# A hybrid decoder trunk in split fp32: weight tiles moved 64 bytes up, and 104 instead of 128 weight columns for the gate unit

## The reference, cut to what matters

```python
def hybrid_layer(x, p_i, ...):
    h = rmsnorm(x, norm_mix)
    z = h @ w_in                     # 1024 x (4*384 + 256 + 4*384 + 2*4)
    (rq, rk, rv, rg, pu, mq, mk, mv, mo, mi, mf) = jnp.split(z, offs, axis=-1)
    y_ret, y_pool, y_ml = retention(...), pool_mix(...), mlstm(..., mi, mf, ...)
    x = x + jnp.concatenate([y_ret, y_pool, y_ml], axis=-1) @ w_out
    h = rmsnorm(x, norm_ffn)
    gu = h @ w_gate_up               # 1024 x 5632
    x = x + (jax.nn.silu(gu[..., :D_FF]) * gu[..., D_FF:]) @ w_down
    hp = rmsnorm(x, norm_ple)
    return x + jax.nn.sigmoid(hp @ w_ple_gate) * (p_i @ w_ple_proj)
```

## Time and profile before

| What | Value |
|---|---|
| Median of 3 runs | 2496.22 us |
| Span of the profiled execution | 2494.5 us |
| What lies around the span, against the median | 1.7 us |
| TensorE matmul busy | 2467.6 us (99%), 11768 records |
| TensorE weight loads busy | 2037.2 us (82%) |
| VectorE, ScalarE, GpSimd busy | 1270.7, 898.2, 992.5 us (51%, 36%, 40%) |
| TensorE in the chain that ended last | 97% |
| Mean granted TensorE clock | 0.998 of full |

### The profile page before, as it was taken

One profiled execution on the slowest core, in us unless ns is written; L12 is line 12 of the kernel. 1 busy time (PEld: TensorE's weight loads), 2 busy tenths in 40 slices (PEclk: granted clock), 3 DMA queues, 4 the chain that ended last, 5 costly groups with the idle time before them and its releaser, 6 DMA issues.

```text
span 2494.5 us, 29698 instructions
## 1 busy us (share of the span) xinstructions
PE 2467.6 (99%) x11768; PEld 2037.2 (82%) x11768; DVE 1270.7 (51%) x1760; ACT 898.2 (36%) x1298; POOL 992.5 (40%) x596
## 2 busy tenths in 40 slices
PE   7999999999999999999999999999999999999998
PEld 6888888888888888888878887888888888888886
DVE  7967845543343352333596777545433433423335
ACT  4333334433333341125333252344433333322253
POOL 3211112278877832321221121223788877222120
PEclk9999999999999999999999999999999999999999
DMA  4342222123223252211143322311232223422111
GB/s 164 105 98 65 71 85 85 45 84 92 76 77 91 87 195 107 78 50 44 38 154 98 78 56 67 102 59 60 80 93 81 76 85 110 150 110 70 51 49 70
DMA packets 89370, 214.43 MB, mean 86 GB/s; under 512 B 34568, under 2 KB 43016, under 8 KB 84880
## 3 DMA queue, kind: packets, MB, share of 16 engines
q1 hardware_dynamic: 61456, 126.90, 16.9%
q10 hardware_dynamic: 27776, 85.63, 10.0%
HBM read 163.70 MB, written 35.68 MB: 80 GB/s over the span
## 4 chain that ended last, share of the span: by engine, by line
PE 97%; DVE 1%; ACT 1%; issue 0%; DMA 0%; POOL 0%; ACTq 0%; DVEq 0%; POOLq 0%
PE proj L1986 20%; PE proj L1987 20%; PE proj L1988 20%; PE proj L2090 5%; PE aux L2090 5%; PE aux L2089 5%; PE proj L2089 5%; PE aux L2088 5%; PE proj L2088 5%; PE aux L2205 1%; PE aux L2224 1%; PE aux L2215 1%; PE aux L2310 0%; PE aux L2315 0%; PE aux L2281 0%; PE aux L2268 0%
## 5 line engine op out<-in xcount | busy, mean ns | idle before, releaser
L1937 POOL TENSOR_TENSOR w_lo<-w_raw,w_hi 128x1024 fp32r<-128x1024 f32 (+1 forms) x144 | 367.2, 2551 | 1256.5 <-ACT w_hi L1468 1256.4
L1986 PE MATMUL proj<-h_hi,w_hi 128*128 128x512 f32 x1760 | 694.8, 395 | 0.9 <-POOL w_lo L1937 0.9
L1988 PE MATMUL proj<-h_lo,w_hi 128*128 128x512 f32 x1760 | 685.5, 389 | 0.0
L1987 PE MATMUL proj<-h_hi,w_lo 128*128 128x512 f32 x1760 | 685.1, 389 | 0.0
L1986 PEld LDWEIGHTS proj<-h_hi,w_hi 128*128 128x128 f32 x1760 | 330.4, 188 | 72.4 <-issue 3.1
L1988 PEld LDWEIGHTS proj<-h_lo,w_hi 128*128 128x128 f32 x1760 | 330.3, 188 | 69.2
L1987 PEld LDWEIGHTS proj<-h_hi,w_lo 128*128 128x128 f32 x1760 | 330.5, 188 | 68.8 <-issue 2.4
L1468 ACT ACTIVATE w_hi<-w_raw 128x1024 fp32r<-128x1024 f32 (+1 forms) x143 | 146.5, 1026 | 440.5 <-PE proj L1988 295.9
L1025 DVE TENSOR_TENSOR x<-x,proj 128x512 f32<-128x512 f32 x128 | 87.7, 687 | 405.6 <-PE proj L1988 405.3
L1944 POOL TENSOR_TENSOR w_lo<-w_raw,w_hi 128x512 fp32r<-128x512 f32 x120 | 183.5, 1531 | 88.5 <-ACT w_hi L1450 88.5
L1944 POOL TENSOR_TENSOR w_lo<-turns,w_hi 128x512 fp32r<-128x512 f32 x120 | 180.4, 1504 | 62.9 <-ACT w_hi L1450 62.9
(11 more groups left out here) (290 smaller groups left out, 4161.3 us busy)
## 6 DMA issues: line engine op xcount, KB each, us to landing
w_raw<-weights SPq DMA_DIRECT2D x168, 512.0 KB, 3.7
act_spill<-act ACTq DMA_DIRECT2D x44, 512.0 KB, 5.5
turns<-weights SPq DMA_DIRECT2D x40, 512.0 KB, 4.4
h_whole<-act_spill ACTq DMA_DIRECT2D x12, 1024.0 KB, 8.1
ffn_b_whole<-act_spill ACTq DMA_DIRECT2D x8, 1024.0 KB, 5.5
w_raw<-weights SPq DMA_DIRECT2D x16, 384.0 KB, 3.1
ml_d<-rows_spill ACTq DMA_DIRECT2D x64, 64.0 KB, 3.4
rows<-ret_qkv ACTq DMA_DIRECT2D x32, 128.0 KB, 2.3
```

The source lines that it names most:

```text
L1937: g.tensor_tensor(wlo[:, slot, 0:n], w, whi[:, slot, 0:n].bitcast(F32), ALU.subtract).then_inc(weights_ready.sem, 1)
L1986: pe.matmul(out, wh, rhi, start=first, stop=False)
L1987: pe.matmul(out, wl, rhi, start=False, stop=False)
L1988: return pe.matmul(out, wh, rlo, start=False, stop=final)
```

## The change

Two edits. A tile of 16 columns (64 bytes) is allocated between `w_raw` and `w_hi`, so `w_hi`, `w_lo` and all that is allocated behind them (`const`, `par`, `early`, `rstd`, `turns`, `rows`, `small` and the rest) begin 64 bytes further up. The arena and `w_raw` stay. And `two_passes` loads 104 columns of weights in place of 128 and writes 104 rows of PSUM; VectorE's three instructions on the result work on 40 rows in place of 64. 104 columns take in the last one used, at 64 + 32 + 3.

```diff
+GATE_ROWS, GATE_COLS = 40, 104
...
         raw = sb("w_raw", [P, 2, 1024])
+        sb("w_gap", [P, 16])
         whi = sb("w_hi", [P, RING, 1024], F32R)
         wlo = sb("w_lo", [P, RING, 1024], F32R)
...
                 if u == U_GATES:
-                    v.tensor_tensor(mix[0:64, 0, sl], src[0:64], scale[0:64], ALU.mult).then_inc(vec_step.sem, 1)
+                    v.tensor_tensor(mix[0:GATE_ROWS, 0, sl], src[0:GATE_ROWS], scale[0:GATE_ROWS],
+                                    ALU.mult).then_inc(vec_step.sem, 1)
                     step_at(L)
-                    src, scale, dst = src[64:128], scale[64:128], mix[0:64, 2, sl]
+                    src, scale, dst = src[64:GATE_COLS], scale[64:GATE_COLS], mix[0:GATE_ROWS, 2, sl]
...
-                v.tensor_tensor(mix[0:64, 0, :], mix[0:64, 0, :], mix[0:64, 2, :], ALU.add).then_inc(vec_step.sem, 1)
+                v.tensor_tensor(mix[0:GATE_ROWS, 0, :], mix[0:GATE_ROWS, 0, :], mix[0:GATE_ROWS, 2, :], ALU.add).then_inc(vec_step.sem, 1)
...
             def two_passes(out, slot, col, rhi, rlo, first, final):
 
-                both = whi[:, slot, col:col + P]
-                pe.matmul(out, both, rhi, start=first, stop=False)
-                return pe.matmul(out, both, rlo, start=False, stop=final)
+                both = whi[:, slot, col:col + GATE_COLS]
+                pe.matmul(out[0:GATE_COLS], both, rhi, start=first, stop=False)
+                return pe.matmul(out[0:GATE_COLS], both, rlo, start=False, stop=final)
```

## The result

The changed kernel is slower: a median of 2560.73 us over 4 runs (2559.99 to 2561.64) against 2497.06 us of the kernel before (4 runs, 2496.17 to 2498.07). The ratio is 1.0256, with a 95% interval of 1.0244 to 1.0268. I had forecast 2445 us. The time is outside the range too, and on the side of rival B.

What follows compares the result with a forecast made beforehand. TensorE's pace was taken as the bound: 10144 fp32r matmuls at 226.9 ns. The terms were 2496.2 - 51 (the 64 bytes) - 0.2 (104 columns) = 2445 us, with a range of 2384 to 2520 us.

Steps and rivals of the forecast that it cites:

- rival B: All fp32r matmuls: the present place is the good one, another could stay at 231.8 ns; 50 us slower, 2546 us, chance 0.22.
- What bounds the kernel: Whole kernel: 10144 fp32r matmuls times 226.9 ns between starts give 2302 us, 92% of the span; TensorE's waits are 16.1 us.
- The 64 bytes: All fp32r weight loads: moving them against the streams saves 5 ns for each of 10144 matmuls, 51 us less.
- The phase: Stretch after a wait: steps of 231.8 ns against 226.9, with only the moment at which loads and streams meet different.
- Where the surplus exists: fp32r matmuls: 13.6 ns over 213.3 ns when the stream reads at full rate; plain fp32 matmuls have only some 3 ns.
- The bound above: fp32r matmuls: at worst the distance rises from 226.9 to 231.8 ns, 4.9 ns each, 50 us more.
- Rival A: fp32r matmuls: the place doesn't matter, each load costs the stream a fixed amount; 2496 us, chance 0.28.
- What else moves: Other tiles moved by 64 bytes (`const`, `par`, `turns`, `rows`, `rstd`): the stage pays nothing; a late weight would cost 0.9 us.
- the sum: Whole kernel: 2496.2 - 51 - 0.2 = 2445 us, with the span 1.7 us under the runs' median.
- 104 columns: Gate unit: loads 21 ns shorter but off the path; 2.6 ns less for each of 64 matmuls, 0.2 us less.
- the sign of a fee by column: Gate unit: a distance some 2.6 ns under its neighbours' if weight columns are paid one by one, no less if not.

Runs made afterwards that it cites:

- e1: The kernel before plus the 64-byte gap ahead of `w_hi` alone, gate unit still loading 128 columns: 2559.82 us, ratio 1.0252.
- e5: The kernel before with the whole arena and all behind it moved by 64 bytes, streams and weight loads alike: 2498.59 us.
- e6: The kernel before with the arena moved by 64 bytes and a pad putting `w_raw` and the weights back at multiples of 2048: 2517.02 us.
- e8: The kernel before with a gap of 256 bytes ahead of `w_hi`: 2496.38 us.
- e7: The kernel before with the 64-byte gap behind `w_lo`, so the split weights stay and `const`, `par` and the rest move: 2496.55 us.
- e2: The changed kernel without its gap, so only the gate unit's 104 columns differ from the kernel before: 2497.17 us, ratio 1.0002.
- e12: The kernel before with a 64-byte gap between `w_hi` and `w_lo`, moving one load in three: 2537.85 us.
- e15: The kernel before with a 192-byte gap between `w_hi` and `w_lo`, moving one load in three: 2538.46 us.

## Why the prediction was wrong

**What bounds the kernel: right.** The number of matmuls times the distance of their starts explains 63.8 of the 65.1 us, with 15.0 us of waits in place of 16.1.

**The step that failed** is the direction in "The 64 bytes": the term of 51 us less, 5 ns for each matmul. It measured 6.4 ns and 63 us more with the gap alone (e1). I took it that the surplus depends on the phase between load and stream, and that both begin at multiples of 512. From there I chose: "the present place, both at multiples of 512, is the one in which the low address bits of load and stream agree", and took agreement for the cause of the surplus. e5, e6 and e8 show the opposite. Agreement modulo 256 is the best of nine places, and the surplus that it leaves is no collision of equal addresses that a shift could clear. The rows allowed either sign. After a wait the stream runs at 231.8 ns and then finds back to 226.9 by itself, so the present placement has a rhythm that it falls into. That was the argument of rival B, to which I gave 0.22. It warned of the loss but couldn't show it: the moved placements have rhythms of their own, and only the runs say that theirs are slower.

**The phase: not what I took it for.** I had read from the earlier trace rows that nothing but the moment at which loads and streams meet is different after a wait. The records don't show that. The weight loads in the same stretch:

```profile
1268.63 0.19 PEld L1988 LDWEIGHTS proj<-h_lo,w_hi 128*128 128x128 f32 x1
...
1271.19 0.19 PEld L1987 LDWEIGHTS proj<-h_hi,w_lo 128*128 128x128 f32 x1
```

They start with the matmuls of the earlier trace rows, at 1268.63 and 1271.18. By the time stamps every load of this stretch begins 2 to 4 ns after a matmul does, while the distances go from 240 to 226 ns, and in the settled FFN blocks it is 3 or 4 ns. Only the load right behind the wait began late, 107 ns into its matmul. With a gap of 64 bytes it is mostly 2 or 3 ns. So how a stream begins can matter for its pace, but what differs from one rhythm to the next isn't a phase that these records tell.

**Where the surplus exists: right, and one more row bears on it.** For a short stretch in the first gate unit, after TensorE had waited 2.13 us, the granted clock is 0.50, the lower level of 1.2 GHz:

```profile
17.40:19.70 2.30, 2.30 (x7) 1.84 (x6) 2.30 (x3) 2.30 (x3) 0.00 (x0) 0.50 0.96 397
```

By the time stamps fp32r matmuls follow each other there after 426 to 427 ns, which is 512 columns at 1.2 GHz with nothing over. The changed kernel has the same 426 to 427 ns in its own such stretch, with the gap and 104 columns. The 13.3 ns, and the part of it that the placement moves, belong to the stream at its full rate. It is a handful of matmuls in each kernel. Some more at 426 to 427 ns stand from 10.02 to 12.58 us of the kernel before, right after TensorE's first wait of 9.46 us, and there the profile gives a granted clock of 1.00, so the clock row doesn't explain every one of them.

**The size.** Rival B's price was 4.9 ns for each matmul and 50 us; measured are 6.4 ns and 64 us. The bound above was the mean of a stretch in which the stream was already settling. The single distances in it, by the time stamps, go up to 240 ns, and with the gap every second one is 236 ns for good, with 231 between. So the stream does settle with the gap, in a slower rhythm, and not "nowhere" as rival B had it. A mean over a settling stretch is no upper bound for another placement's rhythm.

**Rival A: wrong.** The place matters by itself (e1), and neither a fixed fee nor a cost of the change of weights in the array would follow the place. The rule of the Trainium skill, page SBUF — State Buffer, section "Who interferes with whom", of two independent read ports on TensorE, gave no effect at all; the runs show one of 63 us, by the place of the weights against the streams. On the other half of that rule the trace agrees: in the kernel before, 2963 matmuls in a row from 478.7 us on keep to 226 to 228 ns each once settled, whatever the other engines do meanwhile. The 215.8 ns that the Trainium skill gives on its page TensorE: Matmul & The Clock Gate, section "Back-to-back issue gap", was reached by no placement here; the lowest pace that lasts is 226.7 ns. The section gives that formula for an isolated matmul, which I had left out, and some 131 ns for a stream of loads and matmuls of 512 columns, which no run here comes near either.

**What else moves: right.** e7 gives 2496.55 beside 2496.72 us. In the changed kernel GpSimd is busy for 15.44 us in a stretch of 19.60 (600.00 to 619.60), and VectorE's L716 (L713 before) takes 1286 ns in place of 1285. The plain fp32 matmuls keep their pace with `par` moved, as the timeline of the changed kernel shows:

```profile
314.30 3.60 PE L2252 MATMUL aux<-mix,par 128*128 128x512 f32 x8
```

The 3.60 us for eight records are those of the earlier trace rows. What lies around the span is 2.0 to 2.1 us in every run whose span is listed, not the 1.7 of the sum; nothing hangs on it.

**104 columns: right in size, wrong in kind.** e2 is the same within its interval of 0.9993 to 1.0012, so the term of 0.2 us can't be told from nothing. In the first half of e2's unit the load is 20 ns shorter, 168 in place of 188, as forecast (21). As the sign of a fee by column I had named a distance 2.6 ns under that of the neighbours. In the changed kernel the second half of the unit has it: 230.7 ns, 14 steps from 1292.29 to 1295.52 us, beside 233.3. The first half, 15 steps from 1281.01 to 1284.51 us, runs at 233.3 like its neighbours, and without the gap the first half is slower than its neighbours (e2). So the sign doesn't show a fee; with 104 columns the unit has rhythms of its own.

**What stays open.** Why the rhythms are what they are: which resource load and stream share, and why agreement still leaves 13 ns. At 2.4 GHz the paces of 226.7 and 233.3 ns are 544 and 560 clocks, 32 and 48 over the 512 columns; no run says what those are spent on. The runs show that it goes by the difference modulo 256 and by what went before, and no more. Whether a placement exists that beats the 226.7 ns, with `w_hi` and `w_lo` at two different places or with other steps between the 128-column groups, wasn't tried beyond e12 and e15.

## What to carry to other kernels

Where TensorE is full of fp32r matmuls that each load new weights, let weights and streams begin at addresses that agree modulo 256 bytes. That holds as far as tried here, for 128x128 weights and 512 columns: each of the eight other differences cost 0.1 to 2.5%, without a wait to show for it and with loads of 188 or 189 ns in the mean. So a small tile allocated ahead of the weights can cost 63 us of 2496: compare the distance of matmul starts before and after any edit to the allocations. And when a stream returns to its pace after every break, take that pace as one rhythm of this placement. It needn't be the best one (with 16 bytes the streams returned to 233.3 ns, and of the long ones a single one ran at 226.7), and it says nothing about another placement, so a change of the placement is a risk as much as a chance.

## What the runs showed of the hardware that I had not expected

- The place of the weights against the moving operand changes the pace of fp32r matmuls of 512 columns, from 226.7 to 233.3 ns, with the weight load's own duration at 188 or 189 ns in the mean throughout. It depends on the difference modulo 256 bytes: 192 ahead and 64 behind both give 229.0 ns.
- The pace is a rhythm that locks. One kernel (16 bytes) held 226.7 ns for 431 matmuls and 233.3 ns for 2963; another (240 bytes) held 228.3 and 226.7 ns, and the same list of matmuls ran at both paces of the first.
- Loading less can be slower: 64 in place of 128 columns in every third load, 134 in place of 188 ns, and 64 rows of PSUM written by those matmuls, made the kernel 27 us slower.
- At the lower clock level nothing is over: 426 to 427 ns for 512 columns of fp32r at a granted clock of 0.50, with the gap and without it.
- Plain fp32 matmuls aren't touched: 0.43 us from record to record, with the weights in `par` 428 or 492 bytes past a multiple of 2048 and with those in `const` at a multiple of 512 or 64 past it.
